# Attention pairs written out for every engine, a second plan for the first pair, and new places at the stage borders of a decoder layer

## The reference, cut to what matters

```python
h = rms_norm(x, norm_mix)
q, k, v, cb, cc, cu = split(h @ w_in)              # q, k, v: 512 columns each; conv: 3 x 512
q, k = rms_norm per head (q_norm, k_norm)
# stick-breaking attention, strictly causal, z = q.k / 8
A[t, s] = sigmoid(z[t, s]) * prod_{s < j < t} (1 - sigmoid(z[t, j]))
attn = A @ v
conv = cb * causal_conv3(cc * cu, conv_w)
x = x + concat(attn, conv) @ w_out
h = rms_norm(x, norm_ffn)
x = x + (silu(h @ w_gate) * (h @ w_up)) @ w_down
```

## Time and profile before

| what | value |
|---|---|
| median of 3 runs | 2471.56 us (2466.45 to 2473.23) |
| the profiled execution, own time | 2467.11 us |
| its span, first to last instruction | 2465.3 us |
| mean granted TensorE clock | 0.996 |
| PE busy | 98% of the span |
| DVE, ACT, POOL busy | 59%, 47%, 50% |
| HBM traffic | 263 MB read, 123 MB written |

### The profile page before, as it was taken

How to read it: one execution, slowest core, us unless ns; L and a number is a source line. 1 busy time by engine, 2 the same in 40 slices (tenths; PEclk the granted TensorE clock), 3 DMA queues, 4 the chain that set the end, 5 groups by cost and what they waited for, 6 DMA issues and landing times.

```text
span 2465.3 us, 34564 instructions
## 1 busy us (share of the span) xinstructions
PE 2423.8 (98%) x12008; PEld 2023.1 (82%) x12008; DVE 1456.8 (59%) x1499; ACT 1167.8 (47%) x1866; POOL 1238.5 (50%) x882
## 2 busy tenths in 40 slices
PE   8999999999999999999999999999999999999999
PEld 6888878888888888888788888878878888888887
DVE  4444367787677777536665555456646555554554
ACT  4322267777777777423533333334533333333333
POOL 1455366878777777204654545305856545450021
PEclk9999999999999999999999999999999999999999
DMA  6989864443534632444333232486642332325665
GB/s 196 319 285 291 255 183 122 140 114 100 164 95 114 175 112 75 153 135 164 124 115 111 87 122 82 144 269 232 226 165 80 112 128 77 115 94 184 222 216 201
DMA packets 337513, 388.15 MB, mean 157 GB/s; under 512 B 21473, under 2 KB 242785, under 8 KB 335073
## 3 DMA queue, kind: packets, MB, share of 16 engines
q1 hardware_dynamic: 337376, 386.49, 49.7%
HBM read 263.20 MB, written 123.21 MB: 157 GB/s over the span
## 4 chain that ended last, share of the span: by engine, by line
PE 92%; DVE 2%; DMA 2%; issue 1%; ACT 1%; POOL 1%; SPq 0%; ACTq 0%; DVEq 0%; POOLq 0%
PE lay_ps L2549 11%; PE lay_ps L2551 11%; PE lay_ps L2553 11%; PE lay_ps L107 9%; PE lay_ps L108 9%; PE lay_ps L109 9%; PE lay_ps L2579 5%; PE lay_ps L2581 5%; PE lay_ps L2580 5%; PE lay_ps L1363 5%; PE lay_ps L1347 3%; PE lay_ps L1348 3%; PE lay_ps L1370 3%; PE lay_ps L1369 2%; DMA lay_A_over<-in_w_down 1%
## 5 line engine op out<-in xcount | busy, mean ns | idle before, releaser
L2453 POOL TENSOR_TENSOR lay_A<-lay_raw,lay_A 128x512 fp32r<-128x512 f32 x264 | 364.9, 1394 | 384.9 <-ACT lay_A L2079 384.9
L2549 PE MATMUL lay_ps<-lay_B,lay_A 128*128 128x512 f32 x1232 | 481.0, 390 | 3.6 <-ACT lay_s L2101 3.6
L2551 PE MATMUL lay_ps<-lay_B,lay_A 128*128 128x512 f32 x1232 | 480.7, 390 | 0.0
L2553 PE MATMUL lay_ps<-lay_B,lay_A 128*128 128x512 f32 x1232 | 480.6, 390 | 0.0
L1210 DVE TENSOR_TENSOR_SCAN lay_stick<-lay_ps,lay_stick 128x128 f32<-128x128 f32 (+5 forms) x192 | 331.1, 1725 | 140.4 <-ACT lay_ps L1109 138.3
L1269 POOL TENSOR_TENSOR lay_a<-lay_a,lay_stick 128x128 f32<-128x128 f32 (+5 forms) x192 | 281.6, 1473 | 120.5 <-DVE lay_stick L1210 107.9
L2326 DVE TENSOR_TENSOR lay_A<-lay_A_over,lay_A 128x1024 fp32r<-128x1024 f32 x154 | 212.6, 1383 | 173.7 <-ACT lay_A L2123 173.1
L2079 ACT ACTIVATE lay_A<-lay_raw 128x512 fp32r<-128x512 f32 x264 | 162.1, 627 | 298.3 <-DMA lay_raw<-in_w_gate 124.5
L2123 ACT ACTIVATE lay_A<-lay_A_over 128x1024 fp32r<-128x1024 f32 x154 | 163.1, 1060 | 243.6 <-PE lay_ps L2581 201.2
L2549 PEld LDWEIGHTS lay_ps<-lay_B,lay_A 128*128 128x128 f32 x1232 | 232.0, 188 | 52.7 <-issue 2.6
L2553 PEld LDWEIGHTS lay_ps<-lay_B,lay_A 128*128 128x128 f32 x1232 | 232.0, 188 | 48.4
(11 more groups left out here) (148 smaller groups left out, 4954.4 us busy)
## 6 DMA issues: line engine op xcount, KB each, us to landing
hid_ops<-lay_s SPq DMA_DIRECT2D x154, 256.0 KB, 2.1
lay_A_over<-hid_ops SPq DMA_DIRECT2D x154, 256.0 KB, 2.8
lay_w_stage<-in_w_in SPq DMA_DIRECT2D x48, 512.0 KB, 4.7
lay_raw<-in_w_gate SPq DMA_DIRECT2D x22, 1024.0 KB, 5.7
lay_raw<-in_w_up SPq DMA_DIRECT2D x22, 1024.0 KB, 8.1
lay_A_over<-wd_ops SPq DMA_DIRECT2D x88, 256.0 KB, 3.0
lay_A_over<-in_w_down SPq DMA_DIRECT2D x66, 256.0 KB, 4.5
lay_wd_raw<-in_w_down SPq DMA_DIRECT2D x11, 1024.0 KB, 6.7
```

Of the source, the lines that this page charges most:

```text
L2453: nc.gpsimd.tensor_tensor(A[:, j, p, 1, :, :], operand(j, p), A[:, j, p, 0, :, :].bitcast(F32), ALU.subtract).then_inc(lo_done, 1)
L2549: nc.tensor.matmul(ps[:, b, :], A[:, j, p, 0, k, :], B[p][:, 0, k, :], start=first_mm, stop=False, skip_group_check=True)
L2551: nc.tensor.matmul(ps[:, b, :], A[:, j, p, 0, k, :], B[p][:, 1, k, :], start=False, stop=False, skip_group_check=True)
L2553: mm = nc.tensor.matmul(ps[:, b, :], A[:, j, p, 1, k, :], B[p][:, 0, k, :], start=False, stop=last_mm, skip_group_check=True)
```

## The change

The plan becomes a function of two lists, and pair 0 gets its own. `COUNT_0` moves two projection steps of pair 0 to unit 2, one from unit 16 and one from unit 20. `LATE[46]` goes from 0 to 1 in all pairs. The loop over pairs 1 and 2 is written out on SP, ACT, DVE and POOL.

```diff
@@ qkv_stage, sync @@
                 if last:
                     att.load_rows(sp)
+                if last:
+                    store_v(t, b)
                 if not first:
                     sp.wait_ge(qkT_lo_done, 2 * t)
                     store_qk(t - 1, 1 - b)
+                if not last:
+                    store_v(t, b)
@@ qkv_stage, scalar @@
+            nc.scalar.activation(sb["warm"][:, :], cst["eps"][:, 0:1], ACT.Sigmoid)
             x_square(0, 0)
@@ attend_conv_stage @@
-        count = [2, 1, 0, 3, 2, 5, 1, 1, 1, 2, 2, 2, 2, 1, 1, 3, 2, 1, 3, 1, 4, 5, 1, 2,
+    COUNT_0 = [2, 1, 2, 3, 2, 5, 1, 1, 1, 2, 2, 2, 2, 1, 1, 3, 1, 1, 3, 1, 3, 5, 1, 2,
...
+    plans = [plan(COUNT_0, LATE_0)] + [plan(COUNT, LATE)] * (PAIRS - 1)
-        def pairs(eng, body):
-            body(0)
-            with eng.Fori(1, PAIRS - 1) as p:
+        def pairs(body):
+            for p in range(PAIRS):
                 body(p)
-            body(PAIRS - 1)
@@ scalar, body @@
-                    sigmoids(p, n)
                     if is_first(p) and n == 0:
                         rest()
+                    if not is_first(p) or n != 1:
+                        sigmoids(p, n)
+                    if is_first(p) and n == 0:
+                        sigmoids(p, 1)
...
-                    if n in plan.ends:
-                        take(p, plan.ends[n])
+                    behind = plans[p].held[n]
+                    if n in plans[p].ends and not behind:
+                        take(p, plans[p].ends[n])
                     if n >= LAG or not is_first(p):
                         aT_part(p, n - LAG)
+                    if n in plans[p].ends and behind:
+                        take(p, plans[p].ends[n])
@@ vector, body @@
+                    if is_first(p) and n == 0:
+                        rest()
                     if not late:
                         running_product(p, n)
-                    if is_first(p) and n == 0:
-                        rest()
-                    if is_first(p) and n == LAG:
+                    if is_first(p) and n in (LAG, LAG + 2):
+                        dve.wait_ge(opening.v_stored[(n - LAG) // 2], DMA * TILES // 2)
+                    if is_first(p) and n == LAG + 4:
                         for b in range(2):
-                            dve.wait_ge(opening.v_stored[b], DMA * TILES // 2)
                             dve.wait_ge(opening.qkT_stored[b], DMA * TILES)
@@ gpsimd, body: pair 0 makes a_unit(0) ahead of w_split(0, 1) @@
@@ tensor, body @@
-                    scores(p, n)
+                    if not is_first(p) or n != 1:
+                        scores(p, n)
                     if is_first(p) and n == 0:
                         rest(0)
                         rest(1)
+                        scores(p, 1)
@@ ffn_stage, sync @@
-T_AT = (19, 21, 23, 25, 27, 29, 31, 37, 39, 41, 43, 45, 51, 53, 55, 57)
+B_LOAD_AT, Z_AT = 5, (20, 9)
+T_AT = (21, 22, 23, 25, 27, 29, 31, 37, 39, 41, 43, 45, 51, 53, 55, 57)
-                    if R + 1 < HALVES * ROUNDS:
+                    if R != 1 and R + 1 < HALVES * ROUNDS:
                         for j in range(2):
                             load_raw(R + 1, j)
...
                     for n in range(3):
                         store_hid(R, n)
+                    if R == 0:
+                        for j in range(2):
+                            load_raw(2, j)
                     for n in range(4):
                         store_sum(R, n)
...
-                    if e == 9:
+                    if e == Z_AT[G]:
                         load_z(G, 0)
-                    if G == 0 and e - 10 in range(2 * GT):
-                        load_b(2 * (e - 10))
-                        load_b(2 * (e - 10) + 1)
+                    if G == 0 and e - B_LOAD_AT in range(4 * GT):
+                        load_b(e - B_LOAD_AT)
@@ ffn_stage, scalar, opening: square(14) behind hi(0, 2), was behind hi(0, 3) @@
@@ ffn_stage, scalar, rounds: steady = R > 1 and c > 0 @@
                     if c == 0:
-                        hi(R, 10)
-                        hi(R, 11)
-                    if more and c:
+                        for n in range(10, 14):
+                            hi(R, n)
+                    if more and steady:
                         hi(R + 1, 0)
                     keep(R, GATE, 1)
-                    if c == 0:
-                        hi(R, 12)
-                        hi(R, 13)
-                        hi(R + 1, 0)
-                    if more:
+                    if more and steady:
                         hi(R + 1, 1)
-                    if ahead:
+                    if ahead and steady:
                         hi(R + 1, 2)
                     keep(R, UP, 1)
-                    if ahead:
+                    if not steady:
+                        for n in range(3):
+                            hi(R + 1, n)
+                    elif ahead:
                         hi(R + 1, 3)
                         hi(R + 1, 4)
                     keep(R, GATE, 2)
+                    if not steady:
+                        hi(R + 1, 3)
+                        hi(R + 1, 4)
@@ ffn_stage, vector, rounds: where not steady, the P6 sums come behind total(C22) and total(C11) of GATE @@
@@ ffn_stage, vector, steps @@
                     for d, evict in ((D6, evict_w), (D5, evict_22)):
-                        if e == ENDS[d] + OPS:
-                            for t in range(GT):
+                        if e == ENDS[d] + 2:
+                            for t in range(2):
                                 evict(G, t)
                     op_lo(G, e)
+                    for d, evict in ((D6, evict_w), (D5, evict_22)):
+                        if e == ENDS[d] + 2:
+                            for t in range(2, GT):
+                                evict(G, t)
@@ ffn_stage, tensor @@
-                    if G == 0 and n in (0, 2):
+                    if G == 0 and n in (1, 3):
                         ops["transposes"](MIXED - 2 + n // 2)
```

More of the change, by code:

```diff
@@ L1250, in body @@
                         running_product(p, n)
-            pairs(dve, body)
+            pairs(body)
             aT_part(PAIRS - 1, NU - 3)
@@ L1431, in body @@
                         lower_values(q, units[b][0] - 1)
-                    for k, i in plan.held[n]:
+                    for k, i in plans[p].held[n]:
                         project_step(p, k, i)
-            for p in range(PAIRS):
-                body(p)
+            pairs(body)
             transposes(PAIRS - 1, NU - 3)
@@ L2412, in vector @@
                     total(R, GATE, C11)
+                    if not steady:
+                        for j, p in SUMS[4:6]:
+                            sums(R + 1, j, p)
                     if ahead:
```

76 lines of the change are left out of this document (43 added, 33 removed).

## The result

The changed kernel takes 2447.24 us (median of 4 runs, 2446.63 to 2448.13), the one before, measured beside it, 2469.91 us (2466.45 to 2473.23): ratio 0.991, 95% interval 0.9895 to 0.9926. The profiled execution took 2448.13 us with a span of 2446.3, 19.0 us under the span of before.

What follows compares the result with a forecast made beforehand. PE, busy 98% of the span, was the bound; only its idle and half-clock time could be won. Terms A to F sum to 20.4 us: profiled 2467.1 becomes 2446.7, the median about 2451, range 2442 to 2461 us.

Steps and rivals of the forecast that it cites:

- A: Start of attention: last q, k and unit 1's scores earlier, two steps added, until v lands; 5.0 us, ends 3.0 and 10.5.
- C: Loop over pairs written out: no pass back to the loop's head between pairs 1 and 2; 2.5 us, ends 2.0 and 2.7.
- D: Opening of the feed-forward: a product ahead of tile 14's transposes shortens the norm wait and avoids half clock; 3.4 us.
- E: Feed-forward rounds 1 and 11: PE no longer waits for ACT's keep, nor half clock in round 11; 1.4 and 3.8 us.
- B: Ends of the pairs, unit 46: hi parts before the take of y, last step held back; 0.6 us in three pairs, 1.8.
- F: Down projection: fewer loads per step free the first border, 1.3 us; four evictions in halves shorten PE's waits, 1.2 us.
- The table load: Start of attention: ACT's 1.28 us load moves to the program's head, part of 10.5 us available if v did not bind.
- the last step fills the wait: Unit 46 at the pairs' ends: the held-back projection step covers PE's wait for DVE's lo parts, 0.90 us at 479.68.
- v as no bound: Rival, start of attention: stores drain faster, so up to 10.5 us is gained there, total 2445.7 us; chance 0.10.
- Half clock at the new waits: Rival: 1.2 GHz stretches follow waits for v and at the feed-forward's opening, 1.65 us each, 2454.5 or 2456; chance 0.15.
- Absorbed gains: Rival: later v and a delayed norm leave only the written-out loop and round 11, 6.3 us, total 2465; chance 0.09.
- Written-out code: Rival: fetching the unrolled pairs stalls ACT by 2.68 us a time, making the kernel slower, 2480 us; chance 0.04.

## Why the prediction was right, and where it was not

The time, 2451 forecast and 2447.24 measured, is in the range, and faster by over 0.3% was right. The bounds named for A, C, D and E were the ones found. That the sum came so near, 20.4 against 19.0 us, is in part luck: B and F gave 3.8 us less than forecast, while A gave 1.1 us more and the start of the program 0.95 us that nobody had counted, most of it by a clock that rose earlier. By the steps:

- **A, 5.0 forecast, 6.1 measured.** The mechanism is the one given: unit 3's scores at 311.84, v issued at 323.78 and landed 5.8 us later, PE waiting for it. The terms worked out were 4.5 + 1.36 = 5.9 us; the cut to 5.0 for covers lost at units 16 and 20 was not needed, since no wait of PE appears at either. That v lands 1.1 us before the 330.7 of the forecast comes with the 0.9 us by which the whole program was ahead. That v is the bound is shown twice, by the two steps taken away (v used at the same time, 3.96 us of wait) and by v loaded first.
- **The table load** was counted among the 10.5 us that would be had without the bound. With the bound it is worth nothing at this place.
- **B, 1.8 forecast, 0.5 to 0.7 measured.** The step that failed is "the last step fills the wait": it was filling another one of 0.5 us before. In pair 3 the net was right, nothing, but not for the reason given: the forecast read three stretches at half clock where the trace has five, and left out the one at 990 us, whose 1.5 us were won there and 1.3 of them lost again behind it. Nor was this gain the held step's: the kernel with the old unit 46 has the two waits of before there, and no half clock (last section).
- **C, 2.5 and 2.8.** Right. Its upper end, 2.7, did not reckon with half clock behind the pass back, which gave 3.8 in the kernel with the loop.
- **D, 3.4 and 2.9.** PE waits 0.63 + 0.19 us instead of 1.0 + 0.3, and no half clock follows. The gain is smaller nevertheless, for some tenths come back in the first rounds (a new wait of 0.27 us for POOL at 1207.57, for one).
- **E, 1.4 and 3.8; 1.7 and 4.0.** Right. That keep(GATE, 2) just passes held: PE has no wait for ACT's keep. In round 1 the load does it alone.
- **F, 2.5 forecast, 0.0 measured.** At the border 1.6 us, more than the 1.3 forecast, and 0.8 us behind it that I had not counted. Against that stand 0.7 us at e = 4, a landing that varies. The failed step is "two tiles are emptied sooner, the third arrives about when PE does": it arrives 0.7 us later while POOL works. And of the eviction moved forward the wait for x was not looked up: what the moved instruction itself waits for. About 1 us of the shortfall is chance: at the last eviction of the first half this execution lost 2.2 us, the middle one of nine 1.1.
- **From the profiled execution to the median.** The sum gave 2446.7 for a profiled time that was 2448.13, so the sum promised 1.4 us too much. The 4.45 us added because the median of before lay so much higher were wrong: the changed kernel's runs lie within 1.5 us of each other, those of before within 6.8. That is why 2451 was 3.8 us too high although the sum promised too large a gain: two errors of opposite sign.
- **Rivals.** v as no bound is refuted. Half clock at the new waits did not come: granted clock 1.00 behind all of them. At the start of attention the wait was 1.24 us, and v's waits of 1.24 to 1.67 us in eight profiles were followed by none; with 3.96 us it came. The rule cited from the Trainium skill, "TensorE: Matmul & The Clock Gate", section "HAM oscillation — how this bites in real kernels", that a DMA wait between bursts makes the next burst start at half clock, is told there of waits of about 3 to 5 us. The 3.96 us wait agrees with it, and the shorter ones lie outside its example, which the forecast did not weigh when it called this case the likeliest by the rule. The three stretches that the forecast called in agreement followed waits of PE for DVE and ACT, not for a DMA. Absorbed gains were seen at the end of pair 3 alone. Written-out code costs nothing that shows: distances of 168.32 and 168.32 us, where the border without a pass back took 168.44 before.

## What to carry to other kernels

Moving work or an eviction forward gains only what its new neighbours allow: ask what cover it takes from the instruction in front, what runs beside it (a DVE operation of 1.2 us took 2.1 us with POOL at work), and what it must itself wait for. Where a DMA's landing sets the end of a stretch, fill the time before it with work from later, which here also kept the clock up, and look at what the load's issue waits for: here it waited for stores that it did not need. Differences of a microsecond are to be read between matmuls of the same number in two traces, not in the medians, and at more than two traces: one execution can be off by 1.5 us at a single place.

## What was not expected of the hardware

- **The start of the program varies by its clock.** The granted clock first went to 1.00 at 14.6 to 17.8 us in thirteen profiles, though the first projection matmul came at 13.3 to 13.5 us in all of them, with and without the change. The matmul at about 54 us follows it, within 0.1 us also in the two kernels that load the table late (55.42 us where it rose at 17.79, without the early load): 53.94 us where the clock rose at 14.58, 55.30 where it rose at 17.49, 0.47 us a microsecond. That accounts for 0.7 of the 0.95 us at the start in the table above (the clock rose at 15.54 instead of 17.19).
- **Half clock and the idle time before it.** It followed waits of PE of 2.03, 2.2, 2.9, 3.1, 3.24, 3.25 and 3.96 us, and did not follow 1.24 to 1.67, 1.8 with 1.3 behind it, or 1.90 us. But length is not all. At the end of pair 3, in the kernel before and in the one with the old unit 46, PE's waits are the same two:

```profile
987.75 1.17 PE L1363 MATMUL lay_ps<-all_ident,lay_a 128*128 128x128 f32 x8 [0.90 <-DVE lay_aT_lo L1222]
989.88 0.57 PE L1363 MATMUL lay_ps<-all_ident,lay_a 128*128 128x128 f32 x2 [0.97 <-DVE lay_aT_lo L1222]
```

```profile
979.40 1.16 PE L1383 MATMUL lay_ps<-all_ident,lay_a 128*128 128x128 f32 x8 [0.90 <-DVE lay_aT_lo L1238]
981.54 0.41 PE L1383 MATMUL lay_ps<-all_ident,lay_a 128*128 128x128 f32 x2 [0.97 <-DVE lay_aT_lo L1238]
```

  In the first the granted clock is 0.50 for 3.41 us from 989.99 on, in the second it stays at 1.00. What decides is not shown by these runs.
- **Queues hide in landing times.** The same 1 MB load took 5.8 us behind the stores and 8.4 us beside them. The same x for the last eviction made PE lose from nothing to 1.5 us, in kernels with the same code there.
